# Matmuls of constants on TensorE in front of the norms' first panels and of the delta rule

## The reference, cut to what matters

```
x = layer_norm(ALPHA * x + gate * y, ln_g[layer, 0], ln_b[layer, 0])
u = x * (1.0 + scale) + shift
y = jnp.square(jax.nn.relu(u @ mlp_w1[layer] + mlp_b1[layer])) @ mlp_w2[layer] + mlp_b2[layer]
x = layer_norm(ALPHA * x + gate * y, ln_g[layer, 1], ln_b[layer, 1])
...
h = rms_norm_2(x, norm_mix) * (1 + sc_m) + sh_m
(aq, ak, ..., cqkv, cz, ca, cb) = jnp.split(h @ w_in, points, axis=-1)
o_c = gated_delta_net(cqkv, ca, cb, cz, conv_w, A_log, dt_bias, gdn_norm)
x = x + gt_m * (jnp.concatenate([o_a, o_b, o_c], axis=-1) @ w_out)
h = rms_norm_2(x, norm_ffn) * (1 + sc_f) + sh_f
gate, up = jnp.split(h @ w_gate_up, 2, axis=-1)
return x + gt_f * ((jax.nn.silu(gate) * up) @ w_down)
```

## Time and profile before

| | us |
|---|---|
| median of three runs | 2845.76 |
| lowest and highest | 2843.74, 2847.27 |
| the profiled execution, its own time | 2846.41 |
| its span, first to last instruction | 2844.9 |
| TensorE busy (matmuls) | 2679.1 |
| VectorE busy | 1641.0 |
| ScalarE busy | 1101.6 |
| mean granted clock of TensorE | 0.978 |

### The profile page before, as it was taken

How to read it: one execution, slowest core, us unless ns; L and a number is a source line. 1 busy time by engine, 2 the same in 40 slices (tenths; PEclk the granted TensorE clock), 3 DMA queues, 4 the chain that set the end, 5 groups by cost and what they waited for, 6 DMA issues and landing times.

```text
span 2844.9 us, 41544 instructions
## 1 busy us (share of the span) xinstructions
PE 2679.1 (94%) x17136; PEld 2118.3 (74%) x17136; DVE 1641.0 (58%) x2961; ACT 1101.6 (39%) x1916; POOL 9.4 (0%) x21
## 2 busy tenths in 40 slices
PE   5989999989998899998998899999999988999998
PEld 4766888867666688886876667888878766788886
DVE  6588646573555874657556765444465577533334
ACT  3544324234555442423344543322334355422222
POOL 0000000000000000000000000000000000000000
PEclk9999999999999999999998999999999999999999
DMA  6445555533221366563330013444433200232322
GB/s 252 141 135 173 189 185 177 186 119 102 75 75 53 107 204 201 183 206 107 97 119 17 3 53 126 135 146 148 141 117 107 90 3 2 82 101 94 101 96 82
DMA packets 92091, 336.39 MB, mean 118 GB/s; under 512 B 10480, under 2 KB 10736, under 8 KB 91776
## 3 DMA queue, kind: packets, MB, share of 16 engines
q1 hardware_dynamic: 86800, 315.40, 33.8%
q10 hardware_dynamic: 3792, 14.11, 1.4%
q0 software_dynamic: 1312, 4.23, 0.5%
HBM read 331.57 MB, written 2.13 MB: 117 GB/s over the span
## 4 chain that ended last, share of the span: by engine, by line
PE 46%; ACT 4%; DVE 3%; issue 1%; DVEq 0%; ACTq 0%
PE bank L642 12%; PE bank L643 12%; PE bank L644 12%; ACT probs L2262 1%; PE bank L914 1%; PE bank L681 1%; PE bank L682 1%; PE bank L683 1%; PE bank L995 1%; PE bank L899 1%; PE bank L885 1%; PE bank L1115 0%; DVE probs L1614 0%; PE bank L1177 0%; PE bank L968 0%
## 5 line engine op out<-in xcount | busy, mean ns | idle before, releaser
L642 PE MATMUL bank<-in_high,weights_high 128*128 128x512 f32 x1856 | 736.2, 397 | 12.5 <-DVE in_low L1420 8.2
L1271 DVE TENSOR_TENSOR weights_low<-weight_ring,weights_high 128x1024 fp32r<-128x1024 f32 x404 | 493.9, 1224 | 428.9 <-ACT weights_high L2020 428.7
L643 PE MATMUL bank<-in_low,weights_high 128*128 128x512 f32 x1856 | 726.1, 391 | 0.0
L644 PE MATMUL bank<-in_high,weights_low 128*128 128x512 f32 x1856 | 725.8, 391 | 0.0
L2020 ACT ACTIVATE weights_high<-weight_ring 128x1024 fp32r<-128x1024 f32 x404 | 424.3, 1051 | 444.3 <-PE bank L644 302.1
L642 PEld LDWEIGHTS bank<-in_high,weights_high 128*128 128x128 f32 x1856 | 350.2, 189 | 99.5 <-issue 15.6
L643 PEld LDWEIGHTS bank<-in_low,weights_high 128*128 128x128 f32 x1856 | 350.6, 189 | 74.1 <-issue 3.4
L644 PEld LDWEIGHTS bank<-in_high,weights_low 128*128 128x128 f32 x1856 | 350.5, 189 | 73.9
L642 PE MATMUL bank<-hidden_split,weights_high 128*128 128x512 f32 x864 | 337.0, 390 | 0.0
L644 PE MATMUL bank<-hidden_split,weights_low 128*128 128x512 f32 x864 | 336.3, 389 | 0.0
L643 PE MATMUL bank<-hidden_split,weights_high 128*128 128x512 f32 x864 | 336.3, 389 | 0.0
(11 more groups left out here) (386 smaller groups left out, 3277.5 us busy)
## 6 DMA issues: line engine op xcount, KB each, us to landing
weight_ring<-stream SPq DMA_DIRECT2D x597, 512.0 KB, 3.5
mixer_out<-cmp ACTq DMA_DIRECT2D x6, 1024.0 KB, 5.0
hidden<-forget_rows POOLq DMA_DIRECT2D x16, 256.0 KB, 3.7
residual<-x ACTq DMA_DIRECT2D x4, 512.0 KB, 12.3
mixer_out<-cmp SPq DMA_DIRECT2D x2, 1024.0 KB, 6.5
out<-mixer_out ACTq DMA_DIRECT2D x4, 512.0 KB, 2.7
constants<-consts ACTq DMA_DIRECT2D x1, 1821.5 KB, 20.3
silu_c<-c ACTq DMA_DIRECT2D x2, 512.0 KB, 4.3
```

Source lines behind the costliest of these rows:

```text
L642: pe.matmul(bank[:, :], WHI[:, z, cols], high, start=(k == 0), stop=False)
L643: pe.matmul(bank[:, :], WHI[:, z, cols], low, start=False, stop=False)
L644: ins = pe.matmul(bank[:, :], WLO[:, z, cols], high, start=False, stop=(k == ktiles - 1))
L1271: v.tensor_tensor(WLO[:, z, :], ring[:, n % RING, :], WHI[:, z, :].bitcast(F32), ALU.subtract).then_inc(*mark("weights_low", "low", n))
```

## The change

A helper `busy(bank, n)` issues n fp32 matmuls of the constant matrix `ones` (128x128) by the constant `levels` (128x384) into a bank. They wait for nothing of their own, signal nothing, and their result is overwritten by the next matmul into the bank, which starts a new sum. They are put in eleven places, 63 in all: 5 ahead of the pair of `even_out`, 5 in `mlp(0, 1)`, 10 ahead of `fl`, 10 in `mlp(1, 3)`, 7 behind `layer_norm(3)`, 5 ahead of the first pair of each `hybrid` and 5 ahead of the pair of its feed-forward part (four places), and 3 ahead of `rows` of head 0 in each `hybrid` (two places). No other engine's program changes.

```
+        def busy(bank, n):
+            for _ in range(n):
+                pe.matmul(bank[:, 0:384], ones, const("levels"), start=True, stop=True)
...
-        def gemm(key, x, ktiles=KT, ready=None):
+        def gemm(key, x, ktiles=KT, ready=None, idle=0):
             bank = gemm_bank(key)
+            busy(bank, idle)
...
-        def gemm_pair(keys, x, ready, between=lambda k: None):
+        def gemm_pair(keys, x, ready, between=lambda k: None, idle=5):
 
             banks, used = [gemm_bank(key) for key in keys], [PANELS[key][0] for key in keys]
+            busy(banks[0], idle)
             for n in used:
                 pe.wait_ge(*at("low", n))
...
+                    gemm_pair([("up", l, 0, 0), ("up", l, 0, 1)], u_split, lambda k: ("norm_out", "ln", i - 1, k),
+                              idle=10 if i == 3 else 5)
...
-            gemm(("fl",), u_split, ready=lambda k: ("norm_out", "ln", 1, k))
+            gemm(("fl",), u_split, ready=lambda k: ("norm_out", "ln", 1, k), idle=10)
...
                 h, = which
+                if h == 0:
+                    busy(B[5], 3)
                 pe.wait_ge(*(at("gdn_cols", l) if h < 2 else at("gdn_uw", l, h - 2)))
...
         layer_norm(3)
+        busy(B[5], 7)
         for k in range(KT):
             pe.wait_ge(*at("x_square", "in", 0, k))
```

More of the change, by code:

```diff
@@ L768, in mlp @@
                 if half == 0:
-                    gemm_pair([("up", l, 0, 0), ("up", l, 0, 1)], u_split, lambda k: ("norm_out", "ln", i - 1, k))
+                    gemm_pair([("up", l, 0, 0), ("up", l, 0, 1)], u_split, lambda k: ("norm_out", "ln", i - 1, k),
+                              idle=10 if i == 3 else 5)
                 for j in range(2 if half == 0 else 0, HALF):
```

## The result

The changed kernel takes 2831.46 us (median of 4 runs, 2830.44 to 2834.9) where the kernel before took 2844.75 (4 runs beside it): a ratio of 0.995, 95% interval 0.9938 to 0.9961. The profiled execution took 2830.92, of which 2829.5 are its span.

The account below looks back on a forecast made before the run. TensorE, busy 94% of the span, was taken as the bound, with only work at 1.2 GHz behind its waits to win. Gains of 6.0 + 2.2 + 4.2 = 12.4 us from 2846.41 gave 2834 us, range 2828 to 2840.

Parts of the forecast that it names:

- Pairs behind a norm: Six pairs of panels behind norms: with the clock held, step 3 begins earlier, gaining 6.0 us in sum.
- step 3: In a pair behind a norm: begins six matmuls (1.36 us) and a 0.08 us wait after tile 2 is ready.
- Behind `layer_norm(3)`: Eight mean matmuls, paced by TensorE, take 7.13 us at full clock instead of 9.32: gain 2.2 us.
- `fl`: Ten constants ahead of it gain 0, since DVE paces it even at half clock.
- `even_out`: Five constants behind the wait for ACT's eviction: gain 0, bounds 0 and +0.3 us of loss.
- The delta rule: `rows` of heads 0 and 1 in both `hybrid`: 4.0 us instead of 6.30 in the first; gain 4.2 us, bounds 3.0 and 4.7.
- the deduction of 0.2 and 0.3 us for DVE's softmax: In the delta rule: softmax ends 0.1 us behind head 0's new end, so 2.3 and 2.4 us count as 2.1 each.
- the first rival: Untouched half-clock spells, in the delta rule and elsewhere, are redrawn and give 4 to 6 us back: 2839 us; chance 0.12.
- The second: Rival: the clock holds but DVE sets the end of the pairs, leaving 3 us of gain: 2843 us; chance 0.07.
- The third: Rival: constants count for nothing with the clock, which falls while they run: slower, 2854 us; chance 0.06.
- The fourth: Rival: all 65 us of half clock at the eleven places count by half, 32 us gained: 2814 us; chance 0.02.
- the rule of the Trainium skill: Throttled time costs its length times one minus the clock ratio, thus half: 32 us for the eleven places.

Follow-up runs that it names:

- experiment 5: The changed kernel without the ten constants ahead of `fl`, and with the five at a pair between the waits for its two banks: 2830.6 us, ratio 0.995.
- experiment 9: The changed kernel run again unaltered, a repetition with its own profile: 2830.28 us, ratio 0.9946 to the kernel before.
- experiment 1: The changed kernel with only the 3 + 3 constants ahead of the delta rule's `rows` kept: 2840.88 us, ratio 0.9985 to the kernel before.
- experiment 2: The changed kernel without the 3 + 3 constants ahead of the delta rule's `rows`: 2835.37 us, ratio 0.9964 to the kernel before.
- experiment 4: The changed kernel with ten narrow matmuls of 64 x 2 results for each constant matmul: 2891.24 us, ratio 1.0164 to the kernel before.
- experiment 7: The changed kernel with five narrow matmuls of 64 x 2 results for each constant matmul: 2846.04 us, ratio 1.0007 to the kernel before.
- experiment 3: The changed kernel with three constants more at each normed pair (eight, and thirteen in `mlp(1, 3)`): 2834.14 us, ratio 0.996 to the kernel before.
- experiment 6: The kernel of experiment 5 plus eight constants of 128 columns ahead of the first `xt` of each `hybrid`: 2830.58 us.
- experiment 8: The kernel of experiment 5 with 32 two-column matmuls spread over the convolution panel behind them in each `hybrid`: 2832.18 us, ratio 0.9951 to the kernel before.

## Why the prediction was right, point by point

**Pairs behind a norm: right, 0.7 us too much.** Forecast 6.0 us, found 0.6 + 0.6 + 1.0 + 1.0 + 1.2 + 0.9 = 5.3, and 5.3 the second time. The mis-sized term is step 3 "1.44 behind the end of tile 2". In `mlp(1, 3)` tile 2 is ready at 965.14 + 0.75 = 965.89, and step 3 began at 967.45, 1.56 later. The reason stands in the rows: the two distances between L687 were taken as 0.68 each from a stretch in which TensorE doesn't wait. Behind a wait the first matmul takes 0.51 instead of 0.39, and the first distance is 966.75 - 965.94 = 0.81; the second is 0.70. That makes 0.12 a pair, and six of these are the 0.7 us. The step that starts behind a wait has to be costed by a row behind a wait.

**Behind `layer_norm(3)`: right.** 2.2 us forecast and found, twice; nothing took its place. It is also the cleanest row, since TensorE alone paces it.

**`fl`: right.** The longest spell of half clock before, 10 us, was worth nothing: the shift across it is zero with the constants, and also without them in experiment 5.

**`even_out`: right in kind.** The clock fell at 182.7, behind 3.5 us of idle time and 0.7 us of constants, and the five took 5.16 us, not 3.4, and ended late. That the idle time did it is argued from single executions: it held behind 2.9 us of idle in experiment 9 and behind none in experiment 5. By the shift it had cost 0.8 us in the gated norm at 200 us and 0.24 at 216, where the panels behind are added up, against a bound of 0.3; the rest of the +0.9 in the table is 0.3 from the loading at the start and what the norm behind drew. In the repetition nothing was lost. It is the one place where the constants stand behind the wait instead of in it, and experiment 5 shows that this is mended by the order of two lines, for no gain.

**The delta rule: 4.2 us forecast, 5.1 found in `rows`, 5.6 with what the rest of the delta rule drew.** `rows` gained 2.5 and 2.6 us, more than 2.1. The four pieces gave 2.31 us as forecast (6.30 less 3.99), and 2.5 in the second `hybrid` where 2.4 was forecast. What I didn't count is the piece between the heads, transposes that ran at half clock too: 0.41 us before (1518.37 to 1518.78) and 0.26 after (1511.58 to 1511.84), by the same view. What failed is the deduction of 0.2 and 0.3 us for DVE's softmax as next to be late: head 1 follows without a wait. The rest of the delta rule moved by +0.1 and -0.6 us, and in the repetition by -0.7 and -0.1. That is the redrawing of the first rival, in both directions.

**What wasn't in the sum: 3.2 us.** The convolution panels at 1421 and 2172 ran 3.4 us each at half clock before. The stretch view of before and of after around the second:

```profile
2165.00:2180.00 15.00, 15.00 (x130) 11.76 (x129) 5.33 (x9) 5.60 (x9) 0.00 (x0) 0.89 0.22 71
```
```profile
2160.00:2175.00 15.00, 15.00 (x121) 11.56 (x118) 8.23 (x25) 3.99 (x7) 0.00 (x0) 1.00 0.22 70
```

Since TensorE sets the pace there, a spell costs its half, 1.6 us. I counted untouched spells as an uncertainty of 3 us either way, which is the size that came. Both places fell in before and in experiments 1, 2, 4 and 7, one of them in 3, 5, 6 and 9, none in after and 8. All of those with both but experiment 2 have half clock left at the norms; with so few executions, whether there is more in it than chance is not shown. In experiment 2 both fell with all norm places at full clock, so the norms' constants don't prevent it by themselves.

**The closeness of the sum is in part luck.** The places that were costed gave 5.3 + 2.2 + 5.1 = 12.6 us against 12.4, because the pairs' 0.7 us too much and the 0.9 too little of `rows` cancel. And the 3.2 us of the convolution panels, drawn by chance as far as is known, are as much as the profiled execution (2830.92) lies below the 2834.0 worked out for it, 3.1 us. One sign was missed with them: the mean clock came to 0.991, above the 0.986 to 0.990 stated, since spells outside the eleven places shrank by some 13 us as well.

**The rivals.** The first happened with the other sign, and small. The second didn't: in steps 3 to 7 of a pair TensorE doesn't wait for DVE, and the pairs gained. The third, that constants count for nothing with the clock, falls with the ten places at 1.00. Experiment 7 shows how near it was: with another shape of the same occupation the clock does fall while the constants run, only that it then costs next to nothing, as at all places but `even_out` these still end ahead of the tile. The fourth and the rule of the Trainium skill weighed beside it (page "TensorE: Matmul & The Clock Gate", section Terms) would give 32 us by the estimate made there. The half-clock time did vanish at ten of these places, and 12.6 us came back there. Of half-clock time here only what TensorE paces counts by half: the two convolution spells do, 1.6 of 3.4 us, and the 10 us at `fl` count by nothing.

## What to carry to other kernels

Half clock behind a wait costs only the work that TensorE itself paces from there on; read the first step at which it waits again, and count up to it. Filling a wait with matmuls on constants is worth doing where the clock otherwise falls in or just behind the wait; here it took wide ones, standing ahead of the wait, and 0.5 to 0.7 us of lateness in front of a DVE-paced pair was free. Differences of 1 to 3 us between executions come from spells in code that a change doesn't touch, so a gain of a few us must be read at its own place, by the starts of the same instruction in two traces, before the whole is believed.

## What the runs showed that was not expected

That TensorE can be busy without a gap and fall to half clock all the same: 15.2 us busy of 15.2 at clock 0.50, running matmuls of 64 x 2 results (experiment 4), and again with half as many, where the clock fell some 4.6 us into 6.95 us of them (experiment 7). Matmuls on constants of 384 columns at equal length held 1.00 there.

Such a narrow fp32 matmul is anything but free. The view of one line, L618, gives the duration of one record (least, median, largest, ns), for the kernel after and for experiment 7:

```profile
L618 PE MATMUL bank<-constants x126: 485/486/848, 182.0 to 2455.4; 128*128 128x384 f32 x126
```
```profile
L618 PE MATMUL bank<-constants x630: 197/198/248, 179.3 to 2469.0; 128*64 128x2 f32 x158
```

For 192 times fewer columns the record is 2.5 times shorter, and in a group that ran at full clock throughout (experiment 7, ahead of the first `hybrid`'s pair, 25 in 3.08 us) one takes 0.12 us against 0.66, a fifth. Among wide matmuls it is dearer still: four of them between two tiles cost 0.27 us (2.1 / 8) over what they cost in a row (experiment 8).
